# HGRN scores joined two levels at a time, a reordered start and one compression visit in a hybrid decoder layer

## What is computed

```python
h = rms_norm(x, pre_norm[l])
z = jnp.einsum('btd,dn->btn', h, w_in[l])
# HGRN2: f = lb + (1 - lb) * sigmoid(f_logits); logf = log(f); k = 1 - f; by chunks of 64 tokens:
A = jnp.cumsum(lf, axis=2)
o_inter = jnp.einsum('bhtd,bhde->bhte', qq * jnp.exp(A), S)
rel = jnp.where(tri[:, :, None], A[:, :, :, None, :] - A[:, :, None, :, :], -jnp.inf)
att = jnp.einsum('bhtd,bhsd,bhtsd->bhts', qq, kk, jnp.exp(rel))
o_intra = jnp.einsum('bhts,bhse->bhte', att, vv)
# compression: windows of 32 tokens, one every 16 (15 of them), for keys and for values
ck = jnp.einsum('bcpgd,pde->bcge', kc[:, cidx] + pe_k[:, None, :], w_ck)
cv = jnp.einsum('bcpgd,pde->bcge', vc[:, cidx] + pe_v[:, None, :], w_cv)
```

## Time and profile before

| | us |
|---|---|
| median of 3 runs | 491.39 (491.2 to 491.73) |
| profiled execution, its own time | 491.25 |
| its span, first to last instruction | 489.4 |
| PE busy | 474.8 (97%) |
| DVE busy | 359.8 (74%) |
| ACT busy | 255.9 (52%) |
| POOL busy | 157.4 (32%) |

### The profile page before, as it was taken

How to read it: one execution, slowest core, us unless ns; L and a number is a source line. 1 busy time by engine, 2 the same in 40 slices (tenths; PEclk the granted TensorE clock), 3 DMA queues, 4 the chain that set the end, 5 groups by cost and what they waited for, 6 DMA issues and landing times.

```text
span 489.4 us, 9629 instructions
## 1 busy us (share of the span) xinstructions
PE 474.8 (97%) x3938; PEld 462.8 (95%) x3938; DVE 359.8 (74%) x647; ACT 255.9 (52%) x379; POOL 157.4 (32%) x157
## 2 busy tenths in 40 slices
PE   3999999999999999999999999999999999999995
PEld 3999999999899999999999999999999999999995
DVE  4897999899978775989696755888674357655653
ACT  6966635363484555844366444566554245433541
POOL 1072800702800006992067334546645220000000
PEclk9999999999999999999999999999999999999999
DMA  9965553325525485355537235234435535767502
GB/s 298 322 193 176 173 173 93 98 86 173 173 88 172 137 209 173 97 173 174 171 107 239 87 90 168 88 102 158 130 129 173 174 95 192 232 218 255 173 1 86
DMA packets 77030, 76.43 MB, mean 156 GB/s; under 512 B 6783, under 2 KB 75775, under 8 KB 76987
## 3 DMA queue, kind: packets, MB, share of 16 engines
q1 hardware_dynamic: 76699, 75.64, 49.5%
q10 hardware_dynamic: 288, 0.18, 0.2%
HBM read 74.77 MB, written 1.05 MB: 155 GB/s over the span
## 4 chain that ended last, share of the span: by engine, by line
PE 88%; DVE 9%; DMA 1%; issue 1%; ACT 0%; DVEq 0%
PE ps L970 71%; PE ps L1142 3%; DVE WL L603 3%; PE ps L995 2%; PE ps L1094 2%; PE ps L1083 1%; PE ps L1158 1%; DVE R L648 1%; DVE CP L813 1%; DVE R L649 1%; PE ps L1110 1%; DMA R<-x 1%; DVE PM L716 1%; PE ps L1097 1%; PE ps L1112 1%
## 5 line engine op out<-in xcount | busy, mean ns | idle before, releaser
L970 PE MATMUL ps<-hH,WL 128*128 128x256 f32 x696 | 200.6, 288 | 1.0 <-DVE WL L603 1.0
L970 PE MATMUL ps<-hL,WH 128*128 128x256 f32 x696 | 197.7, 284 | 0.0
L970 PE MATMUL ps<-hH,WH 128*128 128x256 f32 x696 | 197.7, 284 | 0.0
L603 DVE TENSOR_TENSOR WL<-W,WH 128x2048 fp32r<-128x2048 f32 x66 | 152.2, 2307 | 16.1 <-PE ps L970 15.7
L420 ACT ACTIVATE WH<-W 128x2048 fp32r<-128x2048 f32 x66 | 124.6, 1889 | 58.4 <-PE ps L970 58.3
L970 PEld LDWEIGHTS ps<-hH,WL 128*128 128x128 f32 x696 | 132.8, 191 | 2.2 <-DVE WL L603 1.2
L970 PEld LDWEIGHTS ps<-hL,WH 128*128 128x128 f32 x696 | 132.8, 191 | 0.8 <-issue 0.7
L970 PEld LDWEIGHTS ps<-hH,WH 128*128 128x128 f32 x696 | 132.8, 191 | 0.0
L381 POOL TENSOR_SCALAR R<-R,st 128x256 f32<-128x256 f32 x32 | 29.2, 923 | 80.1 <-DVE st L782 80.1
L970 PE MATMUL ps<-bH,WL 128*128 128x256 f32 x192 | 54.9, 286 | 0.0
L970 PE MATMUL ps<-bL,WH 128*128 128x256 f32 x192 | 54.3, 283 | 0.0
(11 more groups left out here) (191 smaller groups left out, 756.0 us busy)
## 6 DMA issues: line engine op xcount, KB each, us to landing
W<-w_in SPq DMA_DIRECT2D x49, 1024.0 KB, 5.2
W<-w_branch SPq DMA_DIRECT2D x12, 1024.0 KB, 5.0
W<-w_out SPq DMA_DIRECT2D x4, 1024.0 KB, 5.4
R<-x SPq DMA_DIRECT2D x2, 512.0 KB, 4.6
W<-w_in SPq DMA_DIRECT2D x2, 512.0 KB, 6.7
R<-cmp_w SPq DMA_DIRECT2D x2, 512.0 KB, 8.4
OC<-pool_w SPq DMA_DIRECT2D x4, 256.0 KB, 5.8
R<-x SPq DMA_DIRECT2D x1, 1024.0 KB, 7.2
```

Of the source, the lines that this page charges most:

```text
L603: dve.tensor_tensor(WL[:, s % 2, :, 0:n], W[:, s % 3, :, 0:n], WH[:, s % 3, :, 0:n], ALU.subtract).then_inc(s_lo, 1)
L970: mm = pe.matmul(o, l, r, start=(k == 0 and j == 0 and not (split and c)), stop=(k == KC - 1 and j == 2 and not (split and not c)))
```

## The change

HGRN: the six block sizes become one top level (128, `TOP`), one of 64 (`HALF`) and two joined ones, 16 and 4 (`RADIX`): in each of the latter a key block meets all later blocks of its group of four through up to three copies of the query, so that one matmul has 192 query columns (`OWN` holds the keys, `REACH` the queries). The last level within blocks of 4 stays. Keys are carried as logarithms: ACT takes the Ln of HK, DVE subtracts HA from it, POOL adds the block's edge, and one exponential over 4096 columns gives keys and decays together; DVE then multiplies by queries only. POOL has 12 operations a pair as before, of 128 to 512 columns. The masks change with it: the 128-column block copy, six copies of 96, 64 and 32 columns, each linked to the one before, and a plain copy of 64 x 64. The normalisation of a pair of heads (L639) moves one slab on.

The start: DVE zeroes PM first, and PE makes 18 float32 matmuls of 128 columns on these zeros before the transposes. `first_product` gets a mixed order. Slab 1 waits for WH alone and takes its hH x WL products last.

Compression: the keys' and values' matmuls alternate in one visit at slab 27, the keys' result in partitions 64 to 127.

```diff
-LEVELS = (128, 64, 32, 16, 8, 4)
-NLV = len(LEVELS)
-SMALL_K, SMALL_Q = NLV, NLV + 1
+RADIX = (16, 4)
+STEPS = ((0, 3, 1), (3, 2, 2), (5, 1, 3))
...
-QK = [R[:, 4 + 2 * b:6 + 2 * b, :].rearrange("p a (l h t) -> p (a l) h t", h=2, t=T) for b in range(2)]
+DEC = [R[:, 4 + 2 * b:6 + 2 * b, :].rearrange("p a n -> p (a n)") for b in range(2)]
+TOP = [CVD[:, 2 * b:2 * b + 2, :] for b in range(2)]
+HALF = [d[:, 0:512].rearrange("p (h t) -> p h t", h=2) for d in DEC]
+OWN = [[d[:, 512 + 1280 * r:1024 + 1280 * r].rearrange("p (h t) -> p h t", h=2) for r in range(2)] for d in DEC]
+REACH = [[d[:, 1024 + 1280 * r:1792 + 1280 * r].rearrange("p (h t) -> p h t", h=2) for r in range(2)]
+         for d in DEC]
+SMALL_K = [d[:, 3072:3584].rearrange("p (h t) -> p h t", h=2) for d in DEC]
+SMALL_Q = [d[:, 3584:4096].rearrange("p (h t) -> p h t", h=2) for d in DEC]
...
-ck_out = ps[0:64, 5, 0:GROUPS * NCMP].rearrange("p (g c) -> p g c", g=GROUPS)
+ck_out = ps[64:128, 5, 0:GROUPS * NCMP].rearrange("p (g c) -> p g c", g=GROUPS)
...
-        for i, b in enumerate(LEVELS):
-            n = 2 * T // (2 * b)
-            av = a2.rearrange("p (n w) -> p n w", w=2 * b)
-            dv = QK[p % 2][:, i].rearrange("p h t -> p (h t)").rearrange("p (n w) -> p n w", w=2 * b)
-            edge = av[:, :, b - 1:b].to_broadcast((P, n, b))
-            last = pool.tensor_tensor(dv[:, :, 0:b], edge, av[:, :, 0:b], ALU.subtract)
-            if i:
-                pool.tensor_tensor(dv[:, :, b:2 * b], av[:, :, b:2 * b], edge, ALU.subtract)
+        k2 = HK[:, 2 * p:2 * p + 2, :].rearrange("p h t -> p (h t)")
+        b, n = 64, 2 * T // 128
+        av = a2.rearrange("p (n w) -> p n w", w=2 * b)
+        kv = k2.rearrange("p (n w) -> p n w", w=2 * b)
+        dv = HALF[p % 2].rearrange("p h t -> p (h t)").rearrange("p (n w) -> p n w", w=2 * b)
+        edge = av[:, :, b - 1:b].to_broadcast((P, n, b))
+        pool.tensor_tensor(dv[:, :, 0:b], kv[:, :, 0:b], edge, ALU.add)
+        pool.tensor_tensor(dv[:, :, b:2 * b], av[:, :, b:2 * b], edge, ALU.subtract)
+        for r, b in enumerate(RADIX):
+            n = 2 * T // b
+            av = a2.rearrange("p (n w) -> p n w", w=b)
+            pool.tensor_tensor(OWN[p % 2][r].rearrange("p h (n w) -> p (h n) w", w=b),
+                               k2.rearrange("p (n w) -> p n w", w=b),
+                               av[:, :, b - 1:b].to_broadcast((P, n, b)), ALU.add)
+            aw = a2.rearrange("p (n j w) -> p n j w", j=4, w=b)
+            to = REACH[p % 2][r].rearrange("p h (n j w) -> p (h n) j w", j=6, w=b)
+            for at, count, far in STEPS:
+                pool.tensor_tensor(to[:, :, at:at + count], aw[:, :, far:4],
+                                   aw[:, :, 0:count, b - 1:b].to_broadcast((P, n // 4, count, b)), ALU.subtract)
         mid = RHO[:, p].rearrange("p (n a) -> p n a", a=1).to_broadcast((P, 2 * T // 4, 4))
-        pool.tensor_tensor(QK[p % 2][:, SMALL_K].rearrange("p h (n w) -> p (h n) w", w=4),
+        pool.tensor_tensor(SMALL_K[p % 2].rearrange("p h (n w) -> p (h n) w", w=4),
+                           k2.rearrange("p (n w) -> p n w", w=4), mid, ALU.add)
+        pool.tensor_tensor(SMALL_Q[p % 2].rearrange("p h (n w) -> p (h n) w", w=4),
                            a2.rearrange("p (n w) -> p n w", w=4), mid, ALU.subtract).then_inc(s_sub, 1)
...
+                k = HK[:, 2 * p:2 * p + 2, :]
+                act.activation(k, k, ACT.Ln, scale=-1.0)
                 act.activation(f, f, ACT.Ln).then_inc(s_ln, 1)
...
-                q = QK[p % 2]
-                act.activation(q[:, 0, :, P:T], HA[:, 2 * p:2 * p + 2, P:T], ACT.Exp)
-                act.activation(q[:, 0, :, 0:P], q[:, 0, :, 0:P], ACT.Exp)
-                act.activation(q[:, 1:NLV].rearrange("p l h t -> p (l h t)"),
-                               q[:, 1:NLV].rearrange("p l h t -> p (l h t)"), ACT.Exp)
-                small = q[:, SMALL_K].rearrange("p h t -> p (h t)")
-                act.activation(q[:, SMALL_Q].rearrange("p h t -> p (h t)"), small, ACT.Exp)
-                act.activation(small, small, ACT.Exp, scale=-1.0).then_inc(s_hexp, 1)
+                act.activation(TOP[p % 2][:, :, P:T], HA[:, 2 * p:2 * p + 2, P:T], ACT.Exp)
+                for e in range(2):
+                    act.activation(TOP[p % 2][:, e, 0:P], HK[:, 2 * p + e, 0:P], ACT.Exp,
+                                   bias=HA[:, 2 * p + e, P - 1:P])
+                act.activation(DEC[p % 2], DEC[p % 2], ACT.Exp).then_inc(s_hexp, 1)
...
-                act.wait_ge(s_hmul, 4 * (n - 1))
+                act.wait_ge(s_sub, 2 * (n - 1))
+                act.wait_ge(s_hexp, 2 * (n - 1))
...
-        link(dve.tensor_scalar(HK[:, 2 * p:2 * p + 2, :], OC[:, 2 * p:2 * p + 2, :], -1.0, 1.0,
-                               ALU.mult, ALU.add))
+        link(dve.tensor_scalar(HK[:, 2 * p:2 * p + 2, :], OC[:, 2 * p:2 * p + 2, :], 1.0, -1e-30,
+                               ALU.subtract, ALU.min))
...
+            dve.tensor_tensor(HK[:, 2 * p:2 * p + 2], HK[:, 2 * p:2 * p + 2], HA[:, 2 * p:2 * p + 2], ALU.subtract)
...
-            if s == U0 + 5 + 4 * (h // 2):
+            if s == U0 + 6 + 4 * (h // 2):
...
-                for i, b in enumerate(LEVELS):
-                    ev = QK[h // 2 % 2][:, i, h % 2].rearrange("p (n w) -> p n w", w=2 * b)
-                    kv = HK[:, h].rearrange("p (n w) -> p n w", w=2 * b)
+                e, hp = h // 2 % 2, h % 2
+                for b, to in ((128, TOP), (64, HALF)):
+                    ev = to[e][:, hp].rearrange("p (n w) -> p n w", w=2 * b)
                     qv = HQ[:, h].rearrange("p (n w) -> p n w", w=2 * b)
-                    dve.tensor_tensor(ev[:, :, 0:b], ev[:, :, 0:b], kv[:, :, 0:b], ALU.mult)
                     dve.tensor_tensor(ev[:, :, b:2 * b], ev[:, :, b:2 * b], qv[:, :, b:2 * b], ALU.mult)
-                sk, sq_ = QK[h // 2 % 2][:, SMALL_K, h % 2], QK[h // 2 % 2][:, SMALL_Q, h % 2]
-                dve.tensor_tensor(sk, sk, HK[:, h], ALU.mult)
+                for r, b in enumerate(RADIX):
+                    qv = HQ[:, h].rearrange("p (n j w) -> p n j w", j=4, w=b)
+                    ev = REACH[e][r][:, hp].rearrange("p (n j w) -> p n j w", j=6, w=b)
+                    for at, count, far in STEPS:
+                        dve.tensor_tensor(ev[:, :, at:at + count], ev[:, :, at:at + count], qv[:, :, far:4],
+                                          ALU.mult)
+                sq_ = SMALL_Q[e][:, hp]
                 dve.tensor_tensor(sq_, sq_, HQ[:, h], ALU.mult).then_inc(s_hmul, 1)
...
-                                     ps[:, b0, K_BLOCK:K_BLOCK + P]))
-            for lv in range(1, NLV):
-                b = LEVELS[lv]
-                r = slice(0, b if lv == 1 else P)
-                to = PM[r, u % 2, 0:P].rearrange("p (n w) -> p n w", w=2 * b)[:, :, b:2 * b]
-                c = slice(64 * (lv - 1), 64 * lv)
-                last = dve.copy_predicated(to, K[r, c].bitcast(mybir.dt.uint32).rearrange(
-                    "p (n w) -> p n w", w=b), ps[r, b0, c].rearrange("p (n w) -> p n w", w=b))
-                if lv < NLV - 1:
-                    link(last)
-            last.then_inc(s_hmask, 1)
+                                     ps[:, b0 + 1, P:2 * P]))
+            for r, b in enumerate(RADIX):
+                c = slice(192 * r, 192 * r + 192)
+                to = PM[:, u % 2, 0:P].rearrange("p (n j w) -> p n j w", j=4, w=b)
+                on = K[:, c].bitcast(mybir.dt.uint32).rearrange("p (n j w) -> p n j w", j=6, w=b)
+                src = ps[:, b0, c].rearrange("p (n j w) -> p n j w", j=6, w=b)
+                for at, count, far in STEPS:
+                    link(dve.copy_predicated(to[:, :, far:4], on[:, :, at:at + count], src[:, :, at:at + count]))
+            dve.tensor_copy(PM[0:64, u % 2, 64:P], ps[0:64, b0, 384:448]).then_inc(s_hmask, 1)
...
+    dve.memset(PM[:, :, 0:P], 0.0).then_inc(s_zero, 1)
     dve.memset(st_eps, EPS).then_inc(s_init, 1)
-    dve.memset(PM[:, :, 0:P], 0.0)
...
-        pe.wait_ge(s_lo, s + 1)
+        if s == 1:
+            pe.wait_ge(s_hi, 1)
+        else:
+            pe.wait_ge(s_lo, s + 1)
...
-        order = [(c, k) for c in range(1 if kind == "gate" else 2) for k in range(KC)]
+        order = [(c, k, j) for c in range(1 if kind == "gate" else 2) for k in range(KC) for j in range(3)]
+        mixed = split or s == 1
         if split:
-            order.sort(key=lambda ck: ck[1])
-        for c, k in order:
+            order.sort(key=lambda ckj: ckj[1])
+        if s == 1:
+            order.sort(key=lambda ckj: ckj[2] == 0)
+        for at, (c, k, j) in enumerate(order):
+            if s == 1 and at == 4 * KC:
+                pe.wait_ge(s_lo, s + 1)
...
-        q = QK[p % 2]
-        for lv in range(1, NLV):
-            b = LEVELS[lv]
-            t = q[:, lv, hp, P * i:P * i + P]
-            up = t.rearrange("p (n w) -> p n w", w=2 * b)[:, :, b:2 * b]
```

(49 more changed lines are left out.)

50 lines of the change are left out of this document (27 added, 23 removed).

## The result

The changed kernel took 494.88 us (median of five runs, 493.39 to 495.38) against 491.39, a ratio of 1.0068 with a 95% interval of 1.0051 to 1.0086. The forecast was 486.3, with a range from 484.4 to 489.5, so sign and range were both wrong. The profiled execution took 495.38 us, the highest of the five.

A forecast was written before the change was run, and what follows sets the result against it. TensorE, 97% busy, was taken as the bound, with VectorE second in one stretch. Gains of 1.6 (start), 1.3 (scores and VectorE) and 2.1 (compression) summed to 5.0 us, giving 486.3 from a median of 491.39; range 484.4 to 489.5.

The forecast's parts named there:

- Part 1: Start: matmuls on zeros raise the clock early and a mixed order avoids waits; gain 1.6 us, bounds 0.6 to 1.8.
- the shift is handed on whole: Slabs 2 to 7: TensorE never waits until 52 us and VectorE waited 1.16 us at 51.97, so the start's gain survives.
- Part 2: HGRN scores on TensorE: 192-column matmuls save 0.22 us a unit, 3.5 us over 16 units if TensorE is the bound.
- Part 3: VectorE in HGRN: masks +0.55 a unit, multiplications -1.15 a head, subtraction +0.6 a scan; Parts 2 and 3 together gain 1.3 us.
- -0.1 for PE: Slab 9: GpSimd still holds up head 0's multiplications, so VectorE frees WL no sooner; TensorE loses 0.1 us.
- The gaps ahead of slabs 9, 15 and 17: Sign of being right: TensorE's gaps there grow to 0.9, 1.2 and 2 us and still end with L603.
- nobody but slab 27's ACT read waits for it: Normalisation one slab on: only that ScalarE read waits for its result, and it follows a unit-free slab; no cost counted.
- takes the same 0.9 us out of one slab and into the next: Normalisation one slab on: 0.9 us of VectorE work only changes slab; no cost counted.
- Part 4: Compression in one visit: keys and values run side by side on output halves, 64 records in 2.0 us; gain 2.1 us.
- rival A: Compression: the halves don't run side by side at these stream lengths; 488.2 us, chance 0.24.
- B: VectorE takes more, or the clock rises late at the start; 488.0 us, chance 0.15.
- D: HGRN mask chain bounds all sixteen units if linked copies of short runs cost more; 493.5 us at 0.45 a copy, chance 0.05.

The follow-up runs named there:

- late request: Low halves of each product's weights asked for after two thirds of its records: changed kernel with normalisation back 491.41 us; kernel before with start and one visit 485.31 us.
- a hold that was short: GpSimd's pairs 1 to 3 held until heads 0, 2 and 4 are multiplied, on the changed kernel with normalisation back and low halves asked for late: 485.25 us.

## Why the prediction was wrong, step by step

The four parts, as forecast and as the medians of the runs with and without each have them:

| part | forecast | measured |
|---|---|---|
| start | 1.6 | 1.6 (alone) |
| joined levels | 1.3 | -0.8 (beside start and visit) |
| one visit | 2.1 | 0.8 (alone) |
| normalisation one slab on | 0 | -5.3 (in the changed kernel) |
| sum | 5.0 | -3.7; the change itself -3.5 |

Even the lowest bounds of the three priced parts (0.6, -0.5, 0.2) gave 491.1 us. Nearly all of the 3.8 us above that belongs to the part priced at nothing.

**Part 1, the start: right in size, wrong in "the shift is handed on whole".** 1.6 us forecast, slab 1 at 15.46 (15.5 forecast), transposes 273 ns in the median instead of 421, and 1.6 on the time of the kernel with the start alone. There the shift arrives whole. In the changed kernel 0.1 us is left at slab 7. I took VectorE's 1.16 us of idle time at 51.97 as proof of room for all of slabs 2 to 7, and read it from the kernel in which TensorE was later and GpSimd's pair 0 shorter. In the changed kernel `lo` took 2.93 and 2.83 us there, the subtraction of HA is new (0.69), and slabs 3 to 6 lose the lead. The late request brings it back (slab 7 at 50.12 with the joined levels in), so it was the lateness of the low halves.

**Part 2, the scores: right.** 0.24 us a unit against 0.22.

**Part 3, what VectorE pays: terms right, landing wrong.** Masks +0.55 and multiplications -1.13 are as forecast (-1.15), the subtraction of HA 0.69 for 0.6. GpSimd's pairs 1 to 3 take 1.8 to 2.1 us longer than before (11.5 instead of 9.7 for pair 2), where I had 1.5. On the path the joined levels were to give 1.3 us; they gave 0.25 alone and cost 0.8 beside start and visit. The kernel with the normalisation back against the one with start and visit only shows where, in TensorE's time: -1.2 us from slab 1 to 7, where I had put nothing; -0.9 to slab 9 (forecast -0.1); +1.0 to slab 13 (0.66); -0.3 to slab 17 (-0.8); +1.1 to slab 24 (1.5); and -0.5 to slab 30, again put at nothing. So two steps failed: that the lead passes through slabs 2 to 7 whole, and "-0.1 for PE" at slab 9. At slab 9 it was not the multiplications that came to cost more than before. Head 0's took 7.7 us where they had taken 7.6, which is as I forecast by the rule of the Trainium skill ("SBUF — State Buffer", Who interferes with whom); the trace agrees. (Eight of the nine that GpSimd held up before took 0.70 to 0.82 us, not the 1.18 that I quoted.) What I left out is `lo` of slab 8, just ahead of them, which GpSimd's longer operations now held up as well:

```profile
52.58 2.28 DVE L603 TENSOR_TENSOR WL<-W,WH 128x2048 fp32r<-128x2048 f32 x1
...
52.48 3.02 DVE L623 TENSOR_TENSOR WL<-W,WH 128x2048 fp32r<-128x2048 f32 x1
```

The first line is from before, the second from after; 0.74 of the 0.9 us is here. The gaps ahead of slabs 9, 15 and 17 were forecast at 0.9, 1.2 and 2 and measured 1.44, 1.03 and 1.51.

**The step that decided the sign: "nobody but slab 27's ACT read waits for it".** True of the engines that wait for its result, and I stopped there. What stands behind it in VectorE's own queue waits as well: the branch product (L849, L859), `lo` of slab 29 and the copy for which TensorE waits. The way over ACT's read (L561), for which L849 stood still, adds only 0.31 us. I priced the move at nothing since it "takes the same 0.9 us out of one slab and into the next"; the two operations took 2.69 us beside GpSimd's, where undisturbed ones took 0.86, and Part 4 had taken the values' 1.9 us of TensorE time out from ahead of product 28, at whose end the copy is asked for. With it came 2.0 us of standstill, 3.0 of slow clock, and 0.8 at slab 25: 5.9 in the profiled execution and 5.3 in the medians. I had named what would make the clock rise early and nowhere asked where a new wait might make it fall.

**Part 4, the compression: mechanism right, size wrong.** 64 records in 2.0 us, so rival A is out. I had read the Trainium skill's "TensorEngine Tiling (Array Packing)", Instruction Overhead, as saying that streams of 60 and 64 columns should not pay; the trace doesn't bear that reading out for two halves side by side. But 2.1 us was the saving in TensorE's own work, not on the path. Product 28 came 2 us sooner to a `lo` that was not sooner, and 0.8 was left. The prediction did say that ACT and VectorE wait for the visit's end; it did not ask what product 28 waits for.

**The rivals.** B (VectorE takes more) has the right engine, at the wrong size. D has the right sign by a mechanism that didn't occur: a linked copy still takes 0.26 us. No rival had the late `CSB` copy; the combination of Part 4 with the moved normalisation was never costed.

## What to carry to other kernels

An edit costed at nothing is costed against the slack of the kernel before. If other parts of the same change use that slack, or move the moment at which the result is asked for, the costs don't add: for each operation behind the moved one in its queue for which another engine waits, compare when it is asked for with when it is there, with all parts in. When a saving lies ahead of a product, look at what the product waits for next; here asking for the low halves after two thirds of the records was worth more (3.5 us) than any part of the change. And where two engines held each other up instruction by instruction, shortening the instructions of one gave nothing (7.7 us for 7.6); keeping their work apart in time did, and only with a hold that was short.

## What the runs showed of the hardware

- The granted clock fell to its 1.2 GHz level around short standstills of TensorE in the midst of work: for 6.8 us around a wait of 2.0 us (changed kernel), for 6.8 around waits of 3.9 and 1.5 (normalisation back, late request), and in some runs for 3.4 behind one of 1.0 (visit and normalisation). Waits of 1.1 us (two visits) and of up to 1.5 (slabs 9 and 17 of the changed kernel) had no fall in the profiled runs. The slow stretch of the changed kernel cost 3.0 us, more than its wait.
- Two float32 matmul streams of 60 and 64 columns into the two halves of the output partitions run side by side: 64 records in 2.0 us, as 32 took before.
- Six of VectorE's multiplications (192, 128 and 64 elements wide, twice) took 1.28 us alone and 5.30 beside GpSimd. The 2048-element `lo` took 2.28 us alone and up to 3.12 beside GpSimd.
